# Strassen's scheme for five of 22 weight slabs in the down projections of a float32 transformer kernel

## The reference

```python
def swiglu(h, w_gate, w_up, w_down):
    return (jax.nn.silu(h @ w_gate) * (h @ w_up)) @ w_down
...
        h = rmsnorm(x, norm_ffn_pre[l])
        x = x + rmsnorm(swiglu(h, w_ffn_gate[l], w_ffn_up[l], w_ffn_down[l]), norm_ffn_post[l])
```

## Time and profile before

| | |
|---|---|
| median of 3 runs | 2468.19 us (2466.92 to 2468.32) |
| the profiled execution's own time | 2467.2 us |
| its span, from the first to the last instruction | 2465.4 us |
| PE busy | 2423.6 us, 98% of the span |
| DVE busy | 1665.8 us, 68% |
| ACT busy | 1187.7 us, 48% |
| PE's share of the chain that ended last | 96% |
| the two down projections' matmuls | 2112, of 11198 PE instructions |

### The profile page before, as it was taken

The page is one execution under the profiler, slowest core; times in us unless marked ns, Lnnn a source line. Parts: engine busy times, 40 slices in busy tenths (PEclk is TensorE's granted clock), DMA queues, the critical chain, the costliest instruction groups (busy, mean ns, idle before and its releaser), DMA issues.

```text
span 2465.4 us, 28468 instructions
## 1 busy us (share of the span) xinstructions
PE 2423.6 (98%) x11198; PEld 2010.1 (82%) x11198; DVE 1665.8 (68%) x2149; ACT 1187.7 (48%) x1535; POOL 99.0 (4%) x150
## 2 busy tenths in 40 slices
PE   5999999999999999999999999999999999999998
PEld 4888888888788888888888888888888888888887
DVE  6998988756776676754445678965775766764444
ACT  4757766345544444444343544544544444443332
POOL 1210000000000000000000213000000000000000
PEclk9999999999999999999999999999999999999999
DMA  9997755564555556556555655445556556556553
GB/s 383 367 369 249 256 188 171 195 232 148 177 190 199 191 190 199 191 192 209 196 189 191 194 193 197 157 162 190 178 194 199 188 193 199 188 193 211 193 190 134
DMA packets 189492, 507.03 MB, mean 206 GB/s; under 512 B 17792, under 2 KB 18080, under 8 KB 188080
## 3 DMA queue, kind: packets, MB, share of 16 engines
q1 hardware_dynamic: 177008, 456.92, 55.0%
q0 software_dynamic: 11824, 46.14, 5.1%
q10 hardware_dynamic: 528, 2.16, 0.2%
HBM read 503.06 MB, written 2.10 MB: 205 GB/s over the span
## 4 chain that ended last, share of the span: by engine, by line
PE 96%; DVE 3%; DMA 1%; issue 0%; ACT 0%; SPq 0%; DVEq 0%; ACTq 0%
PE acc L635 30%; PE acc L637 30%; PE acc L636 30%; DVE gate L1699 1%; PE wk L658 1%; DMA raw<-in_ada_w 1%; DVE lo L1722 0%; PE wk L1109 0%; PE wk L1135 0%; PE wk L820 0%; PE wk L859 0%; PE wk L834 0%; DVE lo L1720 0%; PE wk L807 0%; PE wk L903 0%
## 5 line engine op out<-in xcount | busy, mean ns | idle before, releaser
L635 PE MATMUL acc<-hi,h 128*128 128x512 f32 x2592 | 1017.4, 393 | 1.5 <-DVE lo L1720 0.5
L637 PE MATMUL acc<-hi,h 128*128 128x512 f32 x2592 | 1009.3, 389 | 0.0
L636 PE MATMUL acc<-lo,h 128*128 128x512 f32 x2592 | 1008.7, 389 | 0.0
L1722 DVE SCALAR_TENSOR_TENSOR lo<-raw,gcols,hi 128x1024 fp32r<-128x1024 f32 (+1 forms) x464 | 569.1, 1270 | 185.8 <-ACT hi L1183 183.6
L1183 ACT ACTIVATE hi<-raw,gcols 128x1024 fp32r<-128x1024 f32 (+1 forms) x464 | 497.4, 1128 | 381.0 <-PE acc L637 328.5
L1720 DVE TENSOR_TENSOR lo<-raw,hi 128x1024 fp32r<-128x1024 f32 (+1 forms) x388 | 453.6, 1214 | 293.7 <-ACT hi L1183 293.3
L635 PEld LDWEIGHTS acc<-hi,h 128*128 128x128 f32 x2592 | 486.8, 188 | 103.6 <-issue 2.9
L637 PEld LDWEIGHTS acc<-hi,h 128*128 128x128 f32 x2592 | 486.5, 188 | 102.4
L636 PEld LDWEIGHTS acc<-lo,h 128*128 128x128 f32 x2592 | 486.9, 188 | 99.0 <-issue 0.2
L1183 ACT ACTIVATE hi<-raw 128x1024 fp32r<-128x1024 f32 (+1 forms) x388 | 385.1, 1045 | 347.8 <-DMA raw<-in_w_ffn_down 202.0
L635 PE MATMUL acc<-hi,g_hi 128*128 128x512 f32 x704 | 274.1, 389 | 0.0
(11 more groups left out here) (322 smaller groups left out, 1234.1 us busy)
## 6 DMA issues: line engine op xcount, KB each, us to landing
raw<-in_w_ffn_gate SPq DMA_DIRECT2D x176, 512.0 KB, 3.8
raw<-in_w_ffn_up SPq DMA_DIRECT2D x176, 512.0 KB, 4.6
raw<-in_w_ffn_down SPq DMA_DIRECT2D x176, 512.0 KB, 4.8
raw<-in_w_in SPq DMA_DIRECT2D x144, 512.0 KB, 4.8
raw<-in_w_kv SPq DMA_DIRECT2D x64, 512.0 KB, 4.9
ada_raw<-in_ada_w POOLq DMA_DIRECT2D x38, 512.0 KB, 7.5
gate_raw<-in_ada_w POOLq DMA_DIRECT2D x32, 512.0 KB, 6.2
raw<-in_w_out SPq DMA_DIRECT2D x32, 512.0 KB, 5.1
```

Of the source, the lines that this page charges most:

```text
L635: pe.matmul(o, l_hi, w_hi[:, c], start=first, stop=False, skip_group_check=loaded)
L636: pe.matmul(o, l_hi, w_lo[:, c], start=False, stop=False, skip_group_check=loaded)
L637: mm = pe.matmul(o, l_lo, w_hi[:, c], start=False, stop=last, skip_group_check=loaded)
L1722: ins = vec.scalar_tensor_tensor(out=lo[:, r, c], in0=raw[:, r, c], scalar=gcols[:, st.gain, k:k + 1], in1=hi[:, m % HI_SLOTS, c], op0=ALU ...
```

## The change

In the down projections, slabs 3, 6, 9, 12 and 15 of each column group (`SEVEN`) are no longer multiplied as eight block products but as seven, by Strassen's scheme (in a form with 15 additions). The blocks are: activations a11, a21 (k-block 0, token tiles 0 and 1), a12, a22 (k-block 1); weights b11, b12 (k-block 0, column halves 0 and 1), b21, b22 (k-block 1). The seven products are

- into `wk`: a11 b11 (bank 0), s1 (b11 + b12) (bank 1), s2 (b11 + b12 + b22) (bank 2), s3 (b12 + b22) (bank 3),
- into `acc` directly: a12 b21 (bank 0), s4 b22 (bank 1), a22 (b11 + b12 + b22 + b21) (bank 2),

with s1 = a21 - a22, s2 = s1 - a11, s3 = a11 - a21, s4 = a12 + s2. The four products in `wk` accumulate over the five slabs and are combined once per group.

Of this follow the parts:

1. PE: 21 matmuls for such a slab instead of 24.
2. Each such slab takes two entries in the list of slabs: the slab itself (12 matmuls: with b11, b21, b22, and b12 + b22, which overwrites b12) and a "sums" slab of three quarters, which DVE computes into the next place of the ring (9 matmuls). It has no DMA. ACT and DVE split it like any slab, in halves of 768 columns. It takes a place of the five and a slot of the four.
3. DVE `weight_sums`: four additions 128x512 per such slab, before its `lo`; ACT's `hi` of the slab and of the sums slab now wait for them.
4. DVE `side_sums` (group 0 only, kept for group 1): one addition 128x512, four of 128x128; then ACT `side_hi` and DVE `side_lo` (128x512 each) split them. The first one waits until PE has turned the last part of g.
5. DVE `mix_products` before the `lo` of slab 18: five operations 128x512 that combine `wk`; `mix_into_acc` before the `lo` of slab 19: four additions 128x512 into the banks of `acc`. PE waits for them ahead of slab 17's second token tile (banks 2 and 3) and of slab 18's first (banks 0 and 1).
6. PE waits at the first such slab for all of g (before: for the part that it reads).
7. POOL's DMA of `gain_a` waits until slab 18 of group 0 has been used, since `mixed` lies in its place.
8. The scratch output of ACT's squares moves from `gated` to `m_a`, and three unused semaphores go.

```diff
+SEVEN = ((3, 6, 9, 12, 15), (3, 6, 9, 12, 15))
...
+                if st in st_down and s in SEVEN[g]:
+                    slabs.append((st, g, f"sums{s}"))
...
+    MIX_DONE = max(SEVEN[0]) + 1
...
+                if st in st_down and (s, t) in ((MIX_DONE + 1, 1), (MIX_DONE + 2, 0)):
+                    for n in range(2):
+                        pe.wait_ge(acc_loaded[st.bank(t, n)], 8 + 2 * st_down.index(st) + g + 1)
...
+        def seven(l, g, s):
...
+            first, last = s == min(SEVEN[g]), s == max(SEVEN[g])
+            pe.wait_ge(slab_split, m + 1)
+            pe.wait_ge(g_ready, 2 * FG * (l + 1) if first else 2 * FG * l + s + 1)
+            add(wk[:, 0, :], gt(k0, 0), m, 0, first, last)
+            add(acc[:, 0, :], gt(k1, 0), m, 2)
+            pe.wait_ge(side_made, 2 * (len(SEVEN[0]) * l + i) + 2)
+            add(acc[:, 1, :], s4, m, 3)
+            add(wk[:, 3, :], s3, m, 1, first, last).then_inc(slab_used, 1)
+            pe.wait_ge(slab_split, m + 2)
+            add(wk[:, 1, :], s1, m + 1, 0, first, last)
+            add(wk[:, 2, :], s2, m + 1, 1, first, last)
+            add(acc[:, 2, :], gt(k1, 1), m + 1, 2).then_inc(slab_used, 1)
...
+        def weight_sums(m):
...
+            vec.wait_ge(raw_landed[r], LANDED[m])
+            vec.wait_ge(slab_used, m + 1 - RING + 1)
+            step(vec.tensor_tensor(t1, b11, b12, ALU.add))
+            vec.tensor_tensor(b12, b12, b22, ALU.add).then_inc(sums_made, 1)
+            step(vec.tensor_tensor(t2, t1, b22, ALU.add))
+            vec.tensor_tensor(t4, t2, b21, ALU.add).then_inc(sums_made, 1)
+
+        def side_sums(l, i):
...
+            vec.wait_ge(slab_used, number[gu.name, FG - 1, 7] + 1)
+            vec.wait_ge(g_turned, 2 * l + 2)
+            step(vec.tensor_tensor(side[i][:, 0].rearrange("p j c -> p (j c)"), g_hi[:, 2 * s:2 * s + 2, :].rearrange(flat),
+                                   g_lo[:, 2 * s:2 * s + 2, :].rearrange(flat), ALU.add))
+            step(vec.tensor_tensor(s1, a21, a22, ALU.subtract))
+            step(vec.tensor_tensor(s2, s1, a11, ALU.subtract))
+            vec.tensor_tensor(s3, a11, a21, ALU.subtract)
+            vec.tensor_tensor(s4, a12, s2, ALU.add).then_inc(side_made, 1)
...
+        def mix_products(l, g):
+
+            b = mixed[g]
+            vec.wait_ge(slab_used, number[st_down[l].name, g, f"sums{max(SEVEN[g])}"] + 1)
+            step(vec.tensor_copy(b[0][:], wk[:, 0, :]))
+            step(vec.tensor_tensor(b[1][:], wk[:, 2, :], b[0][:], ALU.add))
+            step(vec.tensor_tensor(b[2][:], wk[:, 1, :], b[1][:], ALU.subtract))
+            step(vec.tensor_tensor(b[3][:], wk[:, 3, :], b[1][:], ALU.add))
+            step(vec.tensor_tensor(b[1][:], wk[:, 1, :], b[3][:], ALU.subtract))
+
+        def mix_into_acc(l, g):
+
+            b = mixed[g]
+            vec.wait_ge(slab_used, number[st_down[l].name, g, MIX_DONE] + 1)
+            for n, o in ((2, b[3]), (3, b[1])):
+                vec.tensor_tensor(acc[:, n, :], acc[:, n, :], o[:], ALU.add).then_inc(acc_loaded[n], 1)
+            vec.wait_ge(acc_paused, 2 * l + g + 1)
+            for n, o in ((0, b[0]), (1, b[2])):
+                vec.tensor_tensor(acc[:, n, :], acc[:, n, :], o[:], ALU.add).then_inc(acc_loaded[n], 1)
...
-        pool.wait_ge(slab_used, number["gu0", FG - 1, 7] + 1)
+        pool.wait_ge(slab_used, number["down0", 0, MIX_DONE + 2] + 1)
```

More of the change, by code:

```diff
@@ L119, in build @@
     gain_a = at("gain_a", [P, D], A0 + 24)
+    SIDES_AT = (A0 + 8, A0 + 12, A0 + 4, A0 + 20, S0 + 1)
+    side = [at(f"side{i}", [P, 2, 4, P], kb) for i, kb in enumerate(SIDES_AT)]
+    side_r = [at(f"side_r{i}", [P, 2, 4, P], kb, F32R) for i, kb in enumerate(SIDES_AT)]
+    MIXED_AT = ((A0 + 24, A0 + 26, A0 + 28, A0 + 30), (A0 + 4, A0 + 6, A0 + 20, A0 + 22))
+    mixed = [[at(f"mixed{g}{i}", [P, HALF], kb) for i, kb in enumerate(places)] for g, places in enumerate(MIXED_AT)]
     g_hi = at("g_hi", [P, FT, T], G0, F32R)
@@ L291, in build @@
     for st in (st_rest, st_out, st_pool, st_gu[0], st_down[0], st_k, st_q, st_v, st_o, st_gu[1], st_down[1]):
-        slabs += [(st, g, s) for g in range(st.groups) for s in range(st.slabs)]
+        for g in range(st.groups):
+            for s in range(st.slabs):
+                slabs.append((st, g, s))
+                if st in st_down and s in SEVEN[g]:
+                    slabs.append((st, g, f"sums{s}"))
     number = {(st.name, g, s): m for m, (st, g, s) in enumerate(slabs)}
@@ L295, in build, with is_sums, cols_of, sevens @@
     N_FRONT = number["out", 0, 0]
+    def is_sums(m):
+        return isinstance(slabs[m][2], str)
+    def cols_of(m):
+        return 3 * HALF if is_sums(m) else slabs[m][0].cols
+    def sevens(m):
+        st, g, s = slabs[m]
+        return st_down.index(st) if st in st_down and s in SEVEN[g] else None
+    LANDED, landings = [], [0] + [32] * (RING - 1)
+    for m in range(N_SLABS):
+        landings[m % RING] += 0 if is_sums(m) else 32
+        LANDED.append(landings[m % RING])
+    MIX_DONE = max(SEVEN[0]) + 1
     ADA_COLS = (0, HALF, GW, D + GW, 2 * D, 2 * D + GW)
@@ L405, in build @@
     m_squares = sem("m_squares")
+    sums_made, side_made, side_hi_made, acc_paused = (
+        sem(n) for n in ("sums_made", "side_made", "side_hi_made", "acc_paused"))
     stored = sem("stored")
@@ L633, in product @@
                         l_hi, l_lo = st.lhs(k, t)
-                        loaded = (st.name, g, b) in LOADED
+                        last = last or pauses and kk == st.kt - 1
+                        loaded = (st.name, g, b) in LOADED or st in st_down and s > MIX_DONE + (t == 0)
                         pe.matmul(o, l_hi, w_hi[:, c], start=first, stop=False, skip_group_check=loaded)
@@ L640, in product @@
                         mm.then_inc(slab_used, 1)
+                    elif pauses:
+                        if t == 0 and n == 1:
+                            mm.then_inc(acc_paused, 1)
                     elif last:
@@ L1059, in _, with add, down @@
         pool_product(1, 3, turns(turn, 2, 4))
+        def seven(l, g, s):
+            st, i = st_down[l], SEVEN[0].index(s)
+            m = number[st.name, g, s]
+            k0, k1 = 2 * s, 2 * s + 1
+            s1, s2, s3, s4 = ((side_r[i][:, 0, j, :], side_r[i][:, 1, j, :]) for j in range(4))
+            def add(o, lhs, slab, q, first=False, last=False):
+                c = slice(q * HALF, (q + 1) * HALF)
+                w_hi, w_lo = hi[:, slab % HI_SLOTS, c], lo[:, place(slab) % RING, c]
+                pe.matmul(o, lhs[0], w_hi, start=first, stop=False)
+                pe.matmul(o, lhs[0], w_lo, start=False, stop=False)
+                return pe.matmul(o, lhs[1], w_hi, start=False, stop=last)
+            first, last = s == min(SEVEN[g]), s == max(SEVEN[g])
[10 more added lines that the diff above has]
+            add(acc[:, 2, :], gt(k1, 1), m + 1, 2).then_inc(slab_used, 1)
+        def down(l, g, s):
+            if s in SEVEN[g]:
+                seven(l, g, s)
+            else:
+                product(st_down[l], g, s)
         def ffn(l):
@@ L1086, in ffn @@
             for s in range(1, st_down[l].slabs):
-                product(st_down[l], 0, s)
+                down(l, 0, s)
             for s in range(st_down[l].slabs - (2, 4)[l]):
-                product(st_down[l], 1, s)
+                down(l, 1, s)
         ffn(0)
@@ L1174, in conv @@
             r = place(m) % RING
-            act.wait_ge(raw_landed[r], 32 * (m // RING + (2 if r else 1)))
+            if is_sums(m):
+                act.wait_ge(sums_made, 2 * sum(is_sums(i) for i in range(m + 1)))
+            else:
+                act.wait_ge(raw_landed[r], LANDED[m])
+            if sevens(m) is not None:
+                act.wait_ge(sums_made, 2 * sum(is_sums(i) for i in range(m)) + 1)
             if m >= HI_SLOTS:
@@ L1189, in conv_to, with side_hi @@
             while made[0] <= min(m, N_SLABS - 1):
+                if sevens(made[0]) is not None and slabs[made[0]][1] == 0:
+                    side_hi(sevens(made[0]), SEVEN[0].index(slabs[made[0]][2]))
                 conv(made[0])
                 made[0] += 1
+        def side_hi(l, i):
+            act.wait_ge(side_made, 2 * (len(SEVEN[0]) * l + i) + 1)
+            act.activation(side_r[i][:, 0].rearrange("p j c -> p (j c)"), side[i][:, 1].rearrange("p j c -> p (j c)"), ACT.Copy
+                           ).then_inc(side_hi_made, 1)
         def run(st, evac, post=None):
@@ L1714, in conv @@
             n = 2 if st.gain is None else st.kt
-            w = st.cols // n
+            w = cols_of(m) // n
+            if sevens(m) is not None:
+                vec.wait_ge(sums_made, 2 * sum(is_sums(i) for i in range(m)) + 2)
             for kk in range(n):
@@ L1729, in conv_to, with before @@
                 ada_to(ada_until(made[0]))
+                before(made[0])
                 conv(made[0])
+                if sevens(made[0]) is not None and slabs[made[0]][1] == 0:
```

(26 more changed lines are left out.)

22 lines of the change are left out of this document (15 added, 7 removed).

## The result

| | median us (range, runs) | against before, 95% interval |
|---|---|---|
| before | 2467.70 (2466.92 to 2468.38, 6) | |
| changed | 2454.48 (2453.51 to 2455.45, 6) | 0.9945 (0.9935 to 0.9954) |

The changed kernel is 13.2 us faster; 13.6 less 0.3 was forecast, 2454.4 us. Two repeats beside later experiments gave 2454.12 and 2453.91.

What follows compares the result with a forecast made beforehand. TensorE's instructions were taken as the bound, busy 98% of the span. Profiled execution 2467.2 - 13.6 + 0.3 = 2453.9; with half of the median's 1.0 excess added, 2454.4 us; range 2452 to 2460.

Steps and rivals of the forecast that it cites:

- The gain: Down projections: 3 matmuls fewer in each of 20 slabs, 60 x 0.227 = 13.6 us less, all on TensorE's chain.
- Rival C: TensorE's seven-product slabs: bank changes cost time, 2461 us, or the clock falls, 2549 us; chance 0.04, of this 0.01 clock.
- The prices: VectorE's added operations: 0.69 us per 128x512 addition, 0.29 at 128 columns, 1.8 for a pair of 768-column `lo` halves.
- Slab 3: Group 0, both layers, first tight place: VectorE's `g_lo` done at 15.4 us, wanted at 17.1; 1.7 us in hand, cost 0.
- The steady course: Group 0, one seven-product and two plain slabs: VectorE needs 14.3 of 15.67 us; 5 us in hand at each.
- The mixing: After slab 15, four times: additions into banks 2 and 3 done at 7.4 us, wanted at 8.2; 0.8 us in hand.
- The 0.3 us put down for stalls: Allowance in all for something being late at the four mixings, added to the forecast time.
- the half microsecond put on the profiled execution: Half of the 1.0 us by which the runs' median lies above the profiled execution, added to reach 2454.4 us.
- VectorE's load in a period of group 0: VectorE's work over one seven-product slab and two plain ones: 14.3 of 15.67 us.
- a short one: Period with one plain slab between instead of two, group 0: VectorE's load put at 11.9 of 10.2 us.
- rivals A and B: A: small stalls at two tight places, 1.2 to some 5 us, chance 0.11; B: VectorE becomes the bound, slower, 0.03.
- rival B's even point: Group 0's sums, `lo` and mixing: dearer VectorE operations eat the gain, 6.8 us a layer, at 1.03 us an addition.

## Why the prediction was right, step by step

**The gain.** 60 matmuls at 0.227 us start to start: 6.80 us a layer in the trace. The step in the new slabs, over changing banks, is the same. The first matmuls of slab 3, changed kernel:

```profile
1130.62 0.39 PE L1113 MATMUL wk<-hi,g_hi 128*128 128x512 f32 x1
1130.85 0.39 PE L1114 MATMUL wk<-lo,g_hi 128*128 128x512 f32 x1
1131.08 0.39 PE L1115 MATMUL wk<-hi,g_lo 128*128 128x512 f32 x1
1131.30 0.39 PE L1113 MATMUL acc<-hi,g_hi 128*128 128x512 f32 x1
```

Rival C, a price of changing banks, is out, and the clock stood at 1.00 through both down projections of the changed kernel. Of what the Trainium skill tells ("TensorE: Matmul & The Clock Gate", section on psum-queue depth-cycling) nothing was seen there; the clock did fall in the experiments, but behind real waits, not behind changes of bank.

**The prices.** They held. Durations in the changed kernel's first down projection (count, busy, mean ns):

```profile
L1812 DVE TENSOR_TENSOR lo<-raw,hi 128x768 fp32r<-128x768 f32 x20 | 18.2, 951 | 0.0
L1852 DVE TENSOR_TENSOR raw<-raw 128x512 f32<-128x512 f32 x10 | 6.9, 693 | 0.3
...
L1892 DVE TENSOR_TENSOR acc<-acc,mixed 128x512 f32<-128x512 f32 x4 | 2.6, 694 | 1.9 <-PE acc L675 1.9
...
L1864 DVE TENSOR_TENSOR side<-side 128x128 f32<-128x128 f32 x5 | 1.5, 292 | 0.2
```

0.69 us was taken for the additions into PSUM and within the ring, 0.29 for 128 columns. An estimate by the formula of the Trainium skill ("VectorE: DVE Perf Modes", section "The TRN2 errata") is 0.29 too, and agrees with the measured 0.292.

**Slab 3.** VectorE at the start of layer 0's down projection, which now reads against the earlier trace rows:

```profile
1119.97 0.69 DVE L1862 TENSOR_TENSOR side<-g_hi,g_lo 128x512 f32<-128x512 f32 x1 [3.30 <-PE wk L1148]
...
1124.54 2.36 DVE L1812 TENSOR_TENSOR lo<-raw,hi 128x1024 fp32r<-128x1024 f32 x2
1126.82 0.69 DVE L1872 TENSOR_TENSOR side_r<-side,side_r 128x512 fp32r<-128x512 f32 x1
1127.42 1.28 DVE L2482 TENSOR_TENSOR g_lo<-wk,g_hi 128x512 fp32r<-128x512 f32 x2
```

TensorE's first down matmul is at 1113.38, so the `g_lo` end at 15.3 (15.4 forecast), 1.9 us ahead of slab 3 at 1130.62. The experiment with eight more operations found the same 1.9.

**The steady course.** 5 us in hand was forecast at each such slab. At slab 15 of group 0 it is 4.9: the `lo` is done at 1188.26, and TensorE begins the slab at 1193.18. The DMA of `gain_a`, which now goes out late, lands 4 us before its first use.

**The mixing.** The additions into banks 2 and 3, and TensorE's second token tile of slab 17:

```profile
1204.05 1.29 DVE L1889 TENSOR_TENSOR acc<-acc,mixed 128x512 f32<-128x512 f32 x2
```

```profile
1206.10 0.39 PE L673 MATMUL acc<-hi,g_hi 128*128 128x512 f32 x1
```

0.76 us in hand, 0.8 forecast, and 0.8 in the experiment with four more. The 0.3 us put down for stalls was not spent.

**What was luck.** That the medians meet the forecast within 0.1 us. The traces give 13.6 us where 13.3 was forecast, the runs of the changed kernel spread over 1.9 us, and the 0.3 for stalls and the half microsecond put on the profiled execution were guesses of the same size.

**What was mis-sized.** VectorE's load in a period of group 0 was put at 14.3 us and 11.9 for a short one. From the first activation sums (1119.97) to the next (1134.89) it works 14.92 us without idle time, 1.2 of it `g_lo`: 13.7. The row that ends the period:

```profile
1134.89 0.69 DVE L1862 TENSOR_TENSOR side<-g_hi,g_lo 128x512 f32<-128x512 f32 x1
```

The short one is 11.45. I had added durations where starts count. For the same reason VectorE is busy for 178 us in a down projection where some 185 were forecast. The changed kernel doesn't feel it. It made my expectation for the short periods too long (11 us of delay, 8.1 measured).

And rivals A and B priced a wait as its own length. The experiments show more: 2.12 us of idle cost 2.4, and 3.9 when the clock fell; 3.9 of idle cost 6.5 and 5.8. By these prices rival B's even point, a loss of 6.8 us a layer, would come earlier than at an addition of 1.03 us; no run tests that. How often the clock falls after a wait of a given length isn't settled; one of four waits of 2.12 us in the recorded execution.

## What to carry to other kernels

Where TensorE is busy without a break, count its instructions and price them start to start; other engines' work is free until its order makes one late, as at the mixing, or its sum does, as with one plain slab between. So list for each added operation what is wanted last behind it and how much is in hand; here 0.8 and 1.7 us were found before the run, and adding work until TensorE waited gave 0.8 and 1.9. What isn't urgent goes behind what TensorE waits for: moving one 2.3 us operation behind two additions turned a loss of 0.9 us into a gain of 1.0.

## What the runs showed of the hardware beyond that

A wait of TensorE costs more than its idle time shows. Without a change of clock it is some 0.3 us more (2.4 us for 2.12 of idle), and a late start of 0.2 us can show no idle time at all. And the granted clock can fall: with 3.9 us of idle in both layers, once during the wait and once behind it, after 2.12 us in one of four places, after waits of 1.0 us and less in none of nine; then matmuls stand 0.43 us apart instead of 0.227 for 8 to 12 of them. Near the kernel's start executions of one program differ in the clock as well (0.80 or 1.00 from 40 to 60 us), worth 0.7 to 0.9 us.
